# First tokens' sequence transform in separate passes of high and low parts, and two instead of one of the shift's weight tiles summed by TensorE, between two channel tiles

## What is computed

```
m = silu(cond) @ w_mod + b_mod                    # 1024 x 6144, split in six: sh1, sc1, gt1, sh2, sc2, gt2
a = rms_norm(x, g_norm_mix) * (1 + sc1) + sh1
ag = a.reshape(B, L, 4, 256)
f = fft2(ag, axes=(1, 3), norm="ortho").real      # over tokens, and over the 256 channels of a group
y = f.reshape(B, L, D) @ w_fnet_out
h = x + gt1 * y                                   # and then a conv FFN with sh2, sc2, gt2, and the second block
```

## Time and profile before

| what | us |
|---|---|
| median of three runs | 1459.3 |
| the profiled execution, its own time | 1457.89 |
| its span from first to last instruction | 1456.1 |
| TensorE busy | 1422.5 |
| VectorE busy | 530.8 |
| ScalarE busy | 508.5 |
| GpSimd busy | 788.0 |

### The profile page before, as it was taken

How to read it: one execution, slowest core, us unless ns; L and a number is a source line. 1 busy time by engine, 2 the same in 40 slices (tenths; PEclk the granted TensorE clock), 3 DMA queues, 4 the chain that set the end, 5 groups by cost and what they waited for, 6 DMA issues and landing times.

```text
span 1456.1 us, 21745 instructions
## 1 busy us (share of the span) xinstructions
PE 1422.5 (98%) x8088; PEld 1171.5 (80%) x8088; DVE 530.8 (36%) x716; ACT 508.5 (35%) x719; POOL 788.0 (54%) x1034
## 2 busy tenths in 40 slices
PE   7999999999999999999999999999999999999997
PEld 5887888888888788888888877877788888888887
DVE  6976422222002842222200268885453222221003
ACT  6424433333122523323211367425443332332222
POOL 1763745545555864554555577663466455455543
PEclk9999999999999999999999999999999999999999
DMA  9872432222322232232233222200133323323221
GB/s 365 342 299 94 140 116 100 101 101 86 102 101 87 82 106 101 86 103 98 90 103 96 87 89 71 75 16 3 57 105 101 101 86 101 101 86 103 99 72 58
DMA packets 45705, 156.96 MB, mean 108 GB/s; under 512 B 5328, under 2 KB 8656, under 8 KB 45520
## 3 DMA queue, kind: packets, MB, share of 16 engines
q1 hardware_dynamic: 45648, 156.16, 31.1%
HBM read 154.04 MB, written 2.10 MB: 107 GB/s over the span
## 4 chain that ended last, share of the span: by engine, by line
PE 85%; DVE 7%; issue 3%; ACT 3%; POOL 1%; DMA 0%; DVEq 0%; SPq 0%; POOLq 0%; ACTq 0%
PE ps L1768 27%; PE ps L1770 26%; PE ps L1769 26%; POOL w_lo L544 1%; DVE tri_p L1215 1%; DVE tri_x L1215 1%; PE ps L2234 1%; DVE mid_sq L1218 1%; DVE act_lo L1218 1%; ACT w_hi L740 1%; DVE rAR L1218 0%; PE ps L1788 0%; DVE pads L1215 0%; PE ps L2290 0%; DVE rB L1215 0%
## 5 line engine op out<-in xcount | busy, mean ns | idle before, releaser
L544 POOL TENSOR_TENSOR w_lo<-raw,w_hi 128x256 fp32r<-128x256 f32 x932 | 694.0, 778 | 566.1 <-ACT w_hi L740 565.7
L1768 PE MATMUL ps<-act_hi,w_hi 128*128 128x512 f32 x1328 | 522.5, 393 | 5.2 <-DVE act_lo L1218 2.0
L1770 PE MATMUL ps<-act_hi,w_lo 128*128 128x512 f32 x1328 | 517.0, 389 | 0.0
L1769 PE MATMUL ps<-act_lo,w_hi 128*128 128x512 f32 x1328 | 516.8, 389 | 0.0
L740 ACT ACTIVATE w_hi<-raw 128x1024 fp32r<-128x1024 f32 x233 | 244.8, 1054 | 431.0 <-PE ps L1770 404.1
L1768 PEld LDWEIGHTS ps<-act_hi,w_hi 128*128 128x128 f32 x1328 | 249.3, 188 | 63.6 <-issue 4.5
L1769 PEld LDWEIGHTS ps<-act_lo,w_hi 128*128 128x128 f32 x1328 | 249.4, 188 | 52.1 <-issue 1.4
L1770 PEld LDWEIGHTS ps<-act_hi,w_lo 128*128 128x128 f32 x1328 | 249.3, 188 | 52.1
L1768 PE MATMUL ps<-hid_hi,w_hi 128*128 (+2 forms) x588 | 219.9, 374 | 0.8 <-issue 0.8
L1769 PE MATMUL ps<-hid_lo,w_hi 128*128 (+2 forms) x588 | 219.7, 374 | 0.0
L1770 PE MATMUL ps<-hid_hi,w_lo 128*128 (+2 forms) x588 | 219.7, 374 | 0.0
(11 more groups left out here) (281 smaller groups left out, 991.8 us busy)
## 6 DMA issues: line engine op xcount, KB each, us to landing
raw<-weight_units SPq DMA_DIRECT2D x233, 512.0 KB, 3.5
wm_mid<-mod_units SPq DMA_DIRECT2D x18, 512.0 KB, 7.5
wm_ring<-mod_units SPq DMA_DIRECT2D x14, 512.0 KB, 8.5
wm_early<-mod_units SPq DMA_DIRECT2D x8, 512.0 KB, 7.7
wm_late<-mod_units SPq DMA_DIRECT2D x8, 512.0 KB, 6.8
x_tok<-tokens SPq DMA_DIRECT2D x4, 512.0 KB, 6.2
xT<-tokens_by_channel SPq DMA_DIRECT2D x1, 2048.0 KB, 8.3
result<-act_out SPq DMA_DIRECT2D x16, 128.0 KB, 1.8
```

The source lines that it names most:

```text
L544: ins = nc.gpsimd.tensor_tensor(w_lo[:, slot, c], raw[:, slot, c], w_hi[:, slot, c].bitcast(f32), SUB)
L1768: nc.tensor.matmul(o, wh, xh, start=start, stop=False, **check)
L1769: nc.tensor.matmul(o, wh, xl, start=False, stop=False, **check)
L1770: return nc.tensor.matmul(o, wl, xh, start=False, stop=stop, **check)
```

## The change

The first tile's high part of x is made in two halves of 512 channels by ScalarE, with the scaled table between them. TensorE begins as soon as the first half and the table's high part are there, with 7 matmuls high x high (the fifth to seventh wait for the second half), then 7 with the low part of x, then 7 with the low part of the table. Before, it began when all four parts were there. `x_low(0)` waits for the second half.

The second part: tiles 14 and 15 of the modulation matrix, not 15 alone, are summed by TensorE, in 16 fp32 matmuls. They and the 8 SH1 columns stand between channel tiles 5 and 6, not behind tile 7. VectorE sums two tiles (8 and 9) of the shift ahead of SC1's result, not three, and four (10 to 13) behind `f_sums(0)`, as before (11 to 14). The transfer of `xT`, and the ones that follow it in SyncE's list, wait for `mod_mm` of the shift where they waited for the sum of tile 13.

```diff
-BY_COLUMN = 2 * KT - 1
+BY_COLUMN = 2 * KT - 2
 def sums_through(i):
-    return i + (i < BY_COLUMN)
+    return min(i + 1, BY_COLUMN) if i < 2 * KT else i + 1 - (2 * KT - BY_COLUMN)
...
-                if before == BY_COLUMN:
+                if before is not None and BY_COLUMN <= before < 2 * KT:
                     sp.wait_ge(sem("mod_mm"), mod_turn(SH1))
...
                 if i == 3 * KT - 1:
-                    sp.wait_ge(sem("wm_used"), sums_through(2 * KT - 3))
+                    sp.wait_ge(sem("mod_mm"), mod_turn(SH1))
                     sp.dma_start(xT[:, :, :], a_xt).then_inc(sem("loaded_once"), 16)
...
-                nc.scalar.activation(xn_hi[:, t * D:(t + 1) * D], x_tok[:, t, :], ACT.Copy).then_inc(sem("in_hi"), 1)
+                first = D // 2 if t == 0 else D
+                nc.scalar.activation(xn_hi[:, t * D:t * D + first], x_tok[:, t, 0:first], ACT.Copy).then_inc(sem("in_hi"), 1)
                 after(sem(f"loaded_cs{t}"), 32)
                 after(sem("x_rstd"), t + 1)
                 nc.scalar.activation(cs_hi[:, t * NY:(t + 1) * NY], cs_raw[:, t, :], ACT.Copy, scale=x_ss[:, t:t + 1]).then_inc(sem("in_hi"), 1)
+                if t == 0:
+                    nc.scalar.activation(xn_hi[:, first:D], x_tok[:, 0, first:D], ACT.Copy).then_inc(sem("in_hi"), 1)
...
-                after(sem("in_hi"), 2 * t + 1)
-                tt(xn_lo[:, x], x_tok[:, t, :], xn_hi[:, x].bitcast(f32), SUB)
+                after(sem("in_hi"), 2 * t + 2 if t else 3)
+                tt(xn_lo[:, x], x_tok[:, t, :], xn_hi[:, x].bitcast(f32), SUB, "x_lo")
...
-                last_k = KT - 2 if vv == SH1 else KT - 1
+                last_k = BY_COLUMN - KT - 1 if vv == SH1 else KT - 1
...
-            for i in range(2, KT + 3):
+            for i in range(2, KT + 2):
                 wm(i)
             mod_out(SC1)
...
-            for i in range(KT + 3, BY_COLUMN):
+            for i in range(KT + 2, BY_COLUMN):
                 wm(i)
...
-            for k in range(TT_):
+            def first_block(x, cs, start):
+                for m in range(KT - 1):
+                    if start and m == KT // 2:
+                        after(sem("in_hi"), 3)
+                    nc.tensor.matmul(ps[:, seq_bank(m), :], x[:, m * P:(m + 1) * P], cs[:, 0:NY], start=start, stop=False)
+
+            after(sem("in_hi"), 2)
+            first_block(xn_hi, cs_hi, True)
+            after(sem("x_lo"), 1)
+            first_block(xn_lo, cs_hi, False)
+            after(sem("cs_lo"), 1)
+            first_block(xn_hi, cs_lo, False)
+            for k in range(1, TT_):
                 after(sem("cs_lo"), k + 1)
                 for m in range(KT - 1):
                     seq(m, k)
...
+            def last_columns():
+                for i in range(BY_COLUMN, 2 * KT):
+                    after(wm_full[wm_place[i][1]], 16 * wm_place[i][2])
+                for m in range(KT):
+                    o = LAST_COLUMN + m
+                    for i in range(BY_COLUMN, 2 * KT):
+                        k = i - KT
+                        nc.tensor.matmul(ps[:, 7, o:o + P], wm_buf(wm_place[i][0])[:, m * P:(m + 1) * P], c_silu[:, k:k + 1].to_broadcast([P, P]), start=i == BY_COLUMN, stop=i == 2 * KT - 1)
+                mod_columns(SH1)
+
             after(lo_done, U_DFT + 1)
             for t in range(KT):
+                if t == KT - 2:
+                    last_columns()
...
-            n, flag, turn, _ = wm_place[BY_COLUMN]
-            after(wm_full[flag], 16 * turn)
-            for m in range(KT):
-                nc.tensor.matmul(ps[:, 7, LAST_COLUMN + m:LAST_COLUMN + m + P], wm_buf(n)[:, m * P:(m + 1) * P], c_silu[:, KT - 1:KT].to_broadcast([P, P]), start=True, stop=True)
-            mod_columns(SH1)
             after(sem("f_new"), 3)
             keep_busy(DC_BANK, 3)
```

2 lines of the change are left out of this document (1 added, 1 removed).

## The result

| | before | after |
|---|---|---|
| median, 9 executions each, same chip | 1459.3 (1457.87 to 1461.9) | 1461.7 (1460.11 to 1466.45) |
| ratio | | 1.0027 (95%: 1.0018 to 1.0035) |
| the profiled execution | 1457.89 | 1461.4 |
| its span | 1456.1 | 1459.5 |

The kernel is slower: the median by 2.4 us where 0.9 was forecast, and the interval of the ratio (2.6 to 5.1 us) leaves the forecast's own range out. (The ratio itself stands for 3.9 us, more than the medians' distance.) The profiled executions differ by 3.5 us.

The account below looks back on a forecast made before the run. TensorE, busy 98% of the span, was taken as the bound. Earlier channel tiles -1.79, second tile of columns +1.79 and wait for sum 13 +0.87 gave +0.87 us: 1460.2 against the median 1459.3, range 1458.2 to 1462.6.

Parts of the forecast that it names:

- the forecast's own range: Whole kernel: the main case's change in time, +0.2 to +1.4 us, given a chance of 0.62.
- the first part's gain: First transform: TensorE starts at 7.87 instead of 9.79, 1.92 us earlier, of which 1.79 is left at channel tile 0.
- the rival of a rise at a fixed time (13.99): First transform: clock stays at 1.2 GHz until 13.99, giving +1.7 us, 1461.0; chance 0.17 together with a late table.
- the sum of both parts: Up to the constant column: -1.79 earlier channel tiles, +1.79 second tile of columns, +0.87 wait; in all +0.87 us.
- U2: Start of the second weight unit of w_fnet_out on TensorE: 63.97 before, forecast at 64.84.
- the wait for sum 13: At the SH1 columns: TensorE waits 0.87 us, from 47.01 to 47.88, for VectorE's sum of modulation tile 13.
- what is moved on SyncE: Transfers of xT and those behind it: issued 2.2 us later, cost 0; 2.2 us if it reached a consumer whole.
- "no wait" at the SC1 columns: Near 29 us: TensorE arrives at 29.07, sum of tile 7 is ready at 28.98, so no wait.
- the falling clock: Shift's columns near 47 us: TensorE drops to 1.2 GHz, giving +5.1 us, 1464.4; chance 0.06.
- The prediction's section on the skill: Start of TensorE: time at the lower clock may differ from 4.2 us; only a longer time would show.
- the cap by tile 7: SC1 columns: VectorE's sum of tile 7 ends at 28.98, so a still earlier TensorE start gains nothing more.
- the same distance from there to the end.: From the second unit of w_fnet_out to the kernel's end: time unchanged; wrong if moved by more than 1.5 us.

Follow-up runs that it names:

- cols_end: Changed kernel with both tiles' columns and the SH1 columns put back behind channel tile 7; 1461.71 against 1458.52, ratio 1.0021.
- first_only: Changed kernel with its second part undone: early start, columns and order of sums as before; 1458.88 against 1458.52, ratio 1.0003.
- moved_wide: Kernel before plus the early start, tile 10's sum moved behind f_sums(0), SC1 matmuls 128 columns wide; 1457.97 against 1459.29, ratio 0.9993.
- no_filler: Changed kernel without the three filler matmuls ahead of the constant column; 1460.89, ratio 1.0013.
- wide_sc1: Changed kernel with the 8 SC1 matmuls 128 columns wide instead of one; 1463.59 against 1458.52, ratio 1.0033.
- second_only: Changed kernel with its first part undone: the new columns, TensorE's start as before; 1462.52 against 1458.52, ratio 1.0027.
- first_moved: Kernel before plus the early start, with tile 10's sum moved behind f_sums(0); 1459.53 against 1458.81, ratio 1.0002.
- pad8: Kernel before plus 8 one-column fp32 matmuls (16 records) near 3 us, in TensorE's first wait; 1459.62 against 1458.79, ratio 1.0007.
- pad16: Kernel before plus 16 one-column fp32 matmuls (32 records) in TensorE's first wait; 1460.12, ratio 1.001.
- same_count: Changed kernel without 8 fillers (3 ahead of the constant column, 5 between 110 and 118 us), TensorE's list as long as before; 1459.48 against 1458.12, ratio 1.0006.
- warm_moved: Kernel before plus 8 fp32 matmuls of 248 columns from 2.9 us, and tile 10's sum moved behind f_sums(0); 1459.27, ratio 1.0006.
- warm: Kernel before plus 8 fp32 matmuls of 248 columns into an unused bank from 2.9 us on; 1460.11 against 1458.81, ratio 1.0013.
- filled_moved: first_moved with one filler each ahead of SC1 columns, channel tile 0 and SH1 columns, none ahead of the constant column; 1458.34 against 1458.79, ratio 1.0000.
- filled_two: first_moved with fillers ahead of SC1 columns and channel tile 0, one instead of three ahead of the constant column; 1458.88 against 1458.12, ratio 1.0009.
- filled_after: Changed kernel with fillers ahead of SC1 columns, channel tile 0 and SH1 columns, none ahead of the constant column; 1460.53, ratio 1.0013.
- after_again: Changed kernel timed and profiled again without an edit; 1461.93 against 1458.12, ratio 1.002.

## Why the prediction was wrong

**Right: what bounds the kernel, and the first part's gain.** ScalarE's half took 0.52 us to the next start (forecast 0.53), TensorE began 0.05 us behind its input, and no other part of the first tile was late. The start was 0.2 us better than forecast because the transfers landed 0.2 us earlier. The rate rose at 11.24, 3.6 us behind the first matmul; over the profiles without a matmul ahead of the transform it was 3.1 (`cols_end`) to 6.0 (`first_only`, `moved_wide`). The Trainium skill, page "TensorE: Matmul & The Clock Gate", section "What's actually happening", has the monitor free-running, so that the place of the rise varies; the traces agree. The section gives ±500 ns for it, and here it varied by 2.9 us over the profiles. As a rule the rival of a rise at a fixed time (13.99) is ruled out, by 11.24 and seven others below 12.3. But what it priced does occur: in `first_only`, `no_filler` and `moved_wide` the rate rose at 13.89, 13.45 and 14.37, hardly earlier than before.

**Right: the sum of both parts.** With the clock up, U2 moved by +0.59 (`wide_sc1`) and the wait for sum 13 was 0.64; the forecast was 0.87 for both, and TensorE started 0.3 us earlier in that profile (7.56) than forecast. `second_only` moved it by 2.5 with the start of before. Taken apart: the early start and tile 10's move are worth 0.64 in `first_moved`, and the columns cost more than that.

**Right: nothing comes of what is moved on SyncE.** xT was issued at 51.38 instead of 47.54, and from U2 to 960 us the offset stays within 0.05 us: no consumer was late.

**Wrong, first step: "no wait" at the SC1 columns, and the clock at the upper level behind them.** The forecast had TensorE at the SC1 columns at 29.07 with sum 7 ready at 28.98, and took their 16 records as they had been. In the trace it is there at 28.67, since the transfers were earlier too, waits 0.24, and the clock falls behind them. I had put the falling clock, with a chance of 0.06, into the shift's columns near 47 us, and gave as its argument that no idle stretch lay among thin matmuls before. The same argument applied at 29 us, where I had just worked out that TensorE would arrive within 0.1 us of its input. What the runs showed, by profile:

| TensorE at the SC1 columns | profiles | clock fell between 28 and 45 us |
|---|---|---|
| arrives as before, no wait (before, `second_only`, `pad8`, `pad16`) | 4 | 0 |
| early, one column, no filler, waits 0.19 to 0.58 (changed kernel twice, `cols_end`, `same_count`, `warm_moved`, `warm`) | 6 | 6: five at 31 to 32 us, `warm` at 37 |
| early, one column, no filler, no wait (`first_moved`, `no_filler`, `first_only`) | 3 | 1: `first_only` at 37 |
| early, 128 columns wide, no wait (`wide_sc1`, `moved_wide`) | 2 | 0 |
| early, a filler ahead, no wait (`filled_moved`, `filled_two`) or 0.13 (`filled_after`) | 3 | 0 |

In the five where it fell near 31 to 32 us TensorE was busy 2.92 to 3.31 of the 3.50 us from 28.0; in `warm` it was 3.00, and the clock held there. In `first_only` and `warm`, where it fell at 37, TensorE had stood still for 1.8 and 2.1 us ahead of channel tile 0. In the profiles without a fall it was busy all 3.50, but for `filled_after` with 3.37. So the fall goes with a wait behind which thin work follows; that this is its cause is argued from 18 profiles, and no run has the wait and wide columns together. By the mean clock, which counts falls anywhere, 107 of 166 executions of the four kernels with the old arrival are at 0.998, 8 of 19 of the changed kernel's, and 25 of 99 of all in rows two and three.

Whether an execution has the wait hangs on the start. Of the profiles with the early start, those with a wait had the rise of the rate 3.1 to 3.9 us behind the first matmul, those without one 4.3 to 6.0 (`warm` and `warm_moved` start at the upper rate, and both had the wait). A late rise brings TensorE to the SC1 columns later, as in `no_filler`. The prediction's section on the skill said that through the cap by tile 7 only a longer time at the lower level would show. It was the other way about: the shorter times met the wait, and the clock fell behind it.

The fall costs 1.6 us, and it goes through whole. Channel tile 0 is late by only 0.6 of it, against `wide_sc1` (35.11 and 34.53), because there TensorE waited for that tile anyway. But VectorE's sums hang on the end of the first transform too, sum 13 comes later by the rest, and the SH1 columns start at 49.29 instead of 47.65.

**Wrong, second step: "the same distance from there to the end."** I took the stages behind 75 us as fixed, because the change doesn't touch them. They grew by 0.74 us between 960 and 1050. Every profile with a longer TensorE list (the changed kernel twice, `second_only`, `wide_sc1`, `cols_end`, `no_filler`, `warm`, `warm_moved`, `filled_after`, `pad8`, `pad16`) has such a loss, 0.7 to 2.6 us outside the falls; the six of equal length (`first_only`, `first_moved`, `filled_moved`, `filled_two`, `same_count`, `moved_wide`) have at most 0.36. `pad8` makes it from the kernel before alone, and `same_count` removes it from the changed one. That the list's length, or the place of the later instructions in it, is the cause is shown so. How it acts is not: the gaps that the trace puts down to "issue" in runs of equal matmuls (0.21 at 1000.88, 0.20 at 1033.61) would fit the engine waiting for its own instructions, but no run isolates that, and the trace of `same_count` has an "issue" gap of its own at 1021.51.

The late falls may belong to it, which is not shown. A fall between 1021 and 1033 us, or at 986, lies in six of the eleven profiles with a longer list (the changed kernel's second, `second_only`, `wide_sc1`, `warm_moved`, `pad8`, `pad16`) and in none of the seven others; it takes 1.5 to 2.9 us. Those near 910 us don't follow the list: three profiles of each sort have one. By the mean clock `second_only`, `pad8` and `pad16` have as many executions at 0.998 (18 of 29) as before.

**The sum again.** Early +0.6, the early fall +1.65, late +0.74: 3.0 at 1050 us in the changed kernel's own profile, and 3.4 at its end with the slower last matmuls. Without the early fall it would be 1.7, but that is one execution: the second profile of the same kernel has a late loss of 1.7 alone. The medians' 2.4 lies between; the ratio's interval, 2.6 to 5.1, begins within and reaches beyond. The executions at 0.998 stay partly open. `after_again`'s five lie 2.8 above before's. The early sum of 0.6 and the late loss of 0.7 to 1.7 give 1.3 to 2.3 of it. An execution without the wait is one with a late rise, which costs up to 0.7 more by `no_filler`; no profile of the unedited changed kernel without an early fall was taken, so this is an estimate from the others.

**What was luck.** The median, 1461.7, lies inside the range that the prediction stated, 1458.2 to 1462.6. The high end stood for a fixed rise with the spread above it. What brought the time there was the fall at 31.7 us, the late loss and the last slice, which had no term in the sum.

## What to carry to other kernels

An engine that arrives earlier at a place where it needs another one's result gains only up to that result; where the work around is thin (one-column matmuls, a short wait), being early by 0.2 us went, here, with a fall of TensorE's clock and 1.6 us. Before such a change, look for the first place where the earlier engine meets an input that isn't moved. Wide instead of one-column matmuls there are a remedy still to be tried: both profiles that had them had no wait to stand. When single profiles are compared, look first where the rate rose at the start, since that alone moved a later stage by up to 0.7 us. And compare two traces stretch by stretch to the very end: added instructions, even ones hidden in idle time, can lengthen a stage 900 us behind them.

## What the runs showed of the hardware that was not expected

- 8 one-column fp32 matmuls hidden in TensorE's first wait lengthened the stages between 960 and 1050 us by 1.5 us (`pad8`), 16 of them by 2.6 (`pad16`).
- The rate rose 3.1 to 6.0 us behind the first matmul of the transform, in kernels that differ little there. The granted clock by stretch doesn't show the lower level at the start; the spacing of the matmuls does.
- A fall can go on though TensorE is busy all the while: 31.1 to 37.9 in `cols_end` (3.60 of 3.60 us busy from 31.5), where it was 31.71 to 35.11 after, 31.4 to 34.8 in `warm_moved`, 32.3 to 35.7 in `after_again`.
- A fall near 56 us, while TensorE has to wait for GpSimd anyway, cost little: `first_moved` had one and U2 0.64 ahead of before, `filled_after` had one and U2 0.77 ahead.
